# Two of the four latent tiles of a product-key expert layer computed densely instead of by gathered rows

## What is computed

```python
q = (xb @ w_query).reshape(t, PEER_HEADS, 2, HALF_KEY)            # 8 heads, 2 halves of 128
s = einsum('thik,hink->thin', q, sub_keys)                        # 128 keys for each half
v_half, i_half = top_k(s, 16)
cand = v_half[:, :, 0, :, None] + v_half[:, :, 1, None, :]        # 16 x 16 pairs
top_v, top_pos = top_k(cand, 16)                                  # idx = i * 128 + j of the 16 best
g = softmax(top_v)
act = gelu(einsum('thkd,td->thk', expert_u[idx], xb))
out = einsum('thkd,thk->td', expert_v[idx], g * act)
```

## Time and profile before

| | us |
|---|---|
| median of 3 runs | 3107.46 (3094.66 to 3108.46) |
| profiled execution | 3118.87 |
| its span in the profile | 3117.1 |
| busy in the span: PE / VectorE / GpSimd / ScalarE | 2413.1 / 1793.4 / 1572.6 / 667.5 |
| DMA | 819.86 MB, mean 263 GB/s |

### The profile page before, as it was taken

One profiled execution on the slowest core, in us unless ns is written; L12 is line 12 of the kernel. 1 busy time (PEld: TensorE's weight loads), 2 busy tenths in 40 slices (PEclk: granted clock), 3 DMA queues, 4 the chain that ended last, 5 costly groups with the idle time before them and its releaser, 6 DMA issues.

```text
span 3117.1 us, 23624 instructions
## 1 busy us (share of the span) xinstructions
PE 2413.1 (77%) x7124; PEld 1185.1 (38%) x7124; DVE 1793.4 (58%) x3673; ACT 667.5 (21%) x1493; POOL 1572.6 (50%) x1376
## 2 busy tenths in 40 slices
PE   7988888999999958967557886766766676667667
PEld 1444554444565424754223342322222232222223
DVE  0347677431115775877876656656666666666552
ACT  0114435221111112111212122121212121221122
POOL 0011222210001333874458667777777777777775
PEclk9799999999999979988778998888988888898898
DMA  8411111140655665997689999999999999999997
GB/s 292 145 48 35 30 44 36 66 152 26 229 182 189 201 230 194 381 416 259 220 292 337 336 351 366 382 363 363 366 371 372 374 374 385 369 378 356 360 361 293
DMA packets 285385, 819.86 MB, mean 263 GB/s; under 512 B 24929, under 2 KB 68065, under 8 KB 285153
## 3 DMA queue, kind: packets, MB, share of 16 engines
q0 software_dynamic: 184320, 671.17, 57.5%
q1 hardware_dynamic: 100960, 147.43, 13.7%
HBM read 813.79 MB, written 4.72 MB: 263 GB/s over the span
## 4 chain that ended last, share of the span: by engine, by line
PE 19%; POOL 16%; DMA 9%; issue 6%; DVE 4%; ACT 1%; SPq 0%; ACTq 0%; POOLq 0%
PE bank L917 14%; POOL arena L1290 9%; POOL arena L1279 8%; DMA arena<-in_peer_u,arena 4%; DMA arena<-in_peer_v,arena 3%; PE bank L886 2%; DVE arena L1610 2%; DMA arena<-in_keys 1%; PE bank L729 1%; DVE arena L1627 1%; ACT arena L1202 0%; PE bank L897 0%; PE bank L744 0%; DVE arena L1617 0%; PE bank L562 0%
## 5 line engine op out<-in xcount | busy, mean ns | idle before, releaser
L917 PE MATMUL bank<-arena 128*128 128x512 f32 x2048 | 995.1, 636 | 422.4 <-ACT arena L1202 339.3
L1279 POOL DMA_INDIRECT arena<-in_peer_u,arena x640 | 711.8, 1112 | 734.0 <-DVE arena L1603 297.6
L1610 DVE CUSTOM_DVE_ANT_0 arena<-arena 128x1024 f32<-128x1024 f32 x640 | 771.0, 1224 | 526.1 <-DMA arena<-in_peer_u,arena 525.9
L1290 POOL DMA_INDIRECT arena<-in_peer_v,arena x640 | 745.4, 1165 | 244.2 <-issue 164.1
L917 PEld LDWEIGHTS bank<-arena 128*128 128x128 f32 x2048 | 402.5, 203 | 1003.4 <-issue 604.9
L729 PE MATMUL bank<-arena 128*128 128x512 f32 (+1 forms) x1600 | 564.1, 515 | 14.5 <-DMA arena<-in_w_in 3.8
L729 PEld LDWEIGHTS bank<-arena 128*128 128x128 f32 x1600 | 307.4, 193 | 266.4 <-issue 226.6
L1202 ACT ACTIVATE arena<-shape_consts,arena 128x128 f32<-128x128 f32 x512 | 195.0, 399 | 923.9 <-PE bank L917 642.8
L583 PE MATMUL bank<-arena 128*128 128x512 f32 x384 | 183.9, 626 | 7.8 <-ACT arena L972 6.5
L1627 DVE SCALAR_TENSOR_TENSOR arena<-arena 128x1024 f32<-128x1024 f32 x127 | 163.7, 1289 | 30.1 <-DMA arena<-in_peer_v,arena 29.1
L1259 POOL TENSOR_TENSOR arena<-arena 128x512 f32<-128x512 f32 x40 | 45.4, 1135 | 266.1 <-ACT arena L1020 266.1
(11 more groups left out here) (203 smaller groups left out, 2065.0 us busy)
## 6 DMA issues: line engine op xcount, KB each, us to landing
arena<-in_w_in SPq DMA_DIRECT2D x22, 2048.0 KB, 8.2
arena<-in_w_ada SPq DMA_DIRECT2D x12, 2048.0 KB, 7.8
arena<-in_w_ssd_out SPq DMA_DIRECT2D x8, 2048.0 KB, 7.7
arena<-in_peer_u,arena POOLq DMA_INDIRECT x640, 6.2
arena<-in_peer_v,arena POOLq DMA_INDIRECT x640, 6.3
arena<-in_w_fourier SPq DMA_DIRECT2D x4, 2048.0 KB, 7.5
arena<-in_w_out SPq DMA_DIRECT2D x4, 2048.0 KB, 13.2
arena<-in_w_query SPq DMA_DIRECT2D x4, 2048.0 KB, 7.7
```

The costliest lines, as they stand in the source:

```text
L917: last = mm(bank[i][:, :], diag[:, m % 4, :], vrow[V_SLOT[k]][:, 512 * i:512 * i + 512], start=(h == 0 and m == 0), stop=(h == PH - 1 and ...
L1279: nc.gpsimd.indirect_dma_start(urow[U_SLOT[k]], None, a["peer_u"], bass.IndirectOffsetOnAxis(ap=entries(IDX, k), axis=0)).then_inc(u_in[U_ ...
L1290: nc.gpsimd.indirect_dma_start(vrow[V_SLOT[k]], None, a["peer_v"], bass.IndirectOffsetOnAxis(ap=entries(IDX, k), axis=0)).then_inc(v_in[V_ ...
L1610: V.tensor_tensor_reduce(out=urow[slot], in0=urow[slot], in1=h2c, scale=1.0, scalar=0.0, op0=ALU.mult, op1=ALU.add, accum_out=dots[item % ...
```

## The change

Tiles 1 and 2 (`APART`) stay gathered. Tiles 3 and 4 (`WHOLE`, 256 tokens) go through all 16,384 experts densely:
- `s_block(i)`: for each of the 128 blocks of 128 experts PE makes u-block times h2 of both tiles (8 matmuls of 128x256), ScalarE takes GELU of it into `Aw` (64 blocks at a time fit). u comes as a copy of `peer_u` laid out for this, `peer_ut`, made before launch.
- The gate: selections keep indices i and j and the softmax weight as tables, which PE turns (`turn_tables`). In 32 units of 8 tokens, for each half of the i range: VectorE compares i with a row of numbers (`equal_i`), ScalarE scales by the weight (`weigh_i`), GpSimd makes the one-hot of j (`hot_units`, 8 `tensor_scalar` of 128x128), PE multiplies them, one 64-column matmul a token (`build_unit`), and VectorE multiplies the result into `Aw` (`gate_unit`).
- `v_block(i)`: PE adds `Aw` of block i times v-block (4 matmuls of 128x512) into four banks.

PE's order is: all queries and scores, score blocks of the first half, the build of its gate, then v block and second-half score block in turn 64 times, the second build, 64 v blocks. Blocks of 0.5 MB come over SP's queue into six slots.

For tiles 1 and 2 the sum with v is now made by VectorE (`v_add`), not by PE, with 4 (later, for u, another 4) slots for each; u runs 40 steps ahead of v. GpSimd and VectorE take these 296 steps in fixed portions: 20 beside the selections, 20 before the first build, 1 or 2 in each of the 32 units, 86 between, again 48 in the second build, the rest at the end. The latent queries take whole loads of w_query (jobs `Q0` to `Q3`) and 128x256 matmuls, twice as many. Outputs are stored from ScalarE's queue.

```diff
@@ constants
+APART, WHOLE = (1, 2), (3, 4)
+U_SLOT = [k % 4 for k in range(PICKS + 32)] + [2 + k % 4 for k in range(PICKS + 32, GATHERED)]
+V_SLOT = [k % 4 for k in range(GATHERED)]
+APART_LEAD = 40
+APART_BUILD = [1 + u % 2 for u in range(UNITS)]
+APART_BETWEEN = 86
...
@@ tensor
+            for half in range(2 * PH):
+                queries(half, 0)
+                queries(half, 1)
+                if half >= 2 and half % 2 == 0:
+                    scores(half // 2 - 1)
+            scores(PH - 1)
...
+            def build_unit(g, u):
+                n = UNITS * g + u
+                pe.wait_ge(s("ihot_done"), n + 1)
+                pe.wait_ge(s("jhot_done"), n + 1)
+                if n >= 2:
+                    pe.wait_ge(s("g_done"), n - 1)
+                for t in range(UNIT):
+                    last = mm(bank[6 + u % 2][:, HALF * t:HALF * t + HALF], hot_j[u % 2][:, t, :], hot_i[u % 2][:, t, :],
+                              start=True, stop=True)
+                last.then_inc(s("g_full"), 1)
...
+            for n, i in enumerate(FIRST_ORDER):
+                s_block(i)
+                if n == 58:
+                    turn_tables()
+            pe.wait_ge(s("tw_out"), 1)
+            for u in range(UNITS):
+                build_unit(0, u)
+            pe.wait_ge(s("g_done"), UNITS)
+            for i in SECOND_ORDER:
+                v_block(i)
+                s_block(HALF + i)
+            for u in range(UNITS):
+                build_unit(1, u)
+            pe.wait_ge(s("g_done"), 2 * UNITS)
+            for i in SECOND_ORDER:
+                v_block(HALF + i)
...
@@ gpsimd
+            def rows_of_apart(n):
...
+                    if j < 2 * PICKS:
+                        if j % TOPK == 0:
+                            pool.wait_ge(s("topk_done"), PH + j // TOPK + 1)
+                        if j == 32:
+                            pool.wait_ge(s("out_done"), 16)
+                        u_row(PICKS + j)
+                    if j >= APART_LEAD:
+                        v_row(PICKS + j - APART_LEAD)
+            def hot_units(g, u):
+                n = UNITS * g + u
+                if n >= 2:
+                    pool.wait_ge(s("g_full"), n - 1)
...
+                for t in range(UNIT):
+                    last = nc.gpsimd.tensor_scalar(hot_j[u % 2][:, t, :], iota, turned_w[:, 1, UNIT * u + t:UNIT * u + t + 1],
+                                                   None, ALU.is_equal)
+                last.then_inc(s("jhot_done"), 1)
+            def build(g):
+                hot_units(g, 0)
+                hot_units(g, 1)
+                for u in range(UNITS):
+                    rows_of_apart(APART_BUILD[u])
+                    if u + 2 < UNITS:
+                        hot_units(g, u + 2)
...
@@ vector
+            def equal_i(g, u):
...
+                TT(hot_i[u % 2], iota[:, HALF * g:HALF * g + HALF].unsqueeze(1).broadcast_to([P, UNIT, HALF]),
+                   turned_w[:, 0, UNIT * u:UNIT * u + UNIT].unsqueeze(2).broadcast_to([P, UNIT, HALF]),
+                   ALU.is_equal).then_inc(s("ieq_done"), 1)
+            def gate_unit(g, u):
...
+                part = Aw[:, :, UNIT * u:UNIT * u + UNIT]
+                TT(part, part, bank[6 + u % 2][:, :].rearrange("p (t i) -> p i t", t=UNIT), ALU.mult).then_inc(s("g_done"), 1)
+            def build(g):
+                equal_i(g, 0)
+                equal_i(g, 1)
+                for u in range(UNITS):
+                    apart_steps(APART_BUILD[u])
+                    gate_unit(g, u)
+                    if u + 2 < UNITS:
+                        equal_i(g, u + 2)
+            context_steps(4)
+            for h in range(PH):
+                top(3 * PH + h)
+                top(4 * PH + h)
+                context_steps(CTX_BESIDE[h])
+                if h in APART_TOP_BESIDE:
+                    top(PH + APART_TOP_BESIDE[h])
+                apart_steps(APART_BESIDE[h])
+            result(0, pv_c, row(3, 0), 1, 0)
+            apart_steps(SOFTMAX_AT)
+            weigh_whole()
+            apart_steps(APART_EARLY - SOFTMAX_AT)
+            dve.wait_ge(s("tw_out"), 1)
+            build(0)
+            apart_steps(APART_BETWEEN)
+            build(1)
+            apart_steps(ASTEPS)
```

More of the change, by code:

```diff
@@ L519, in _ @@
+            for n in range(len(BLOCKS)):
+                load_block(n)
+            sp.wait_ge(s("out_done"), 16 * NT)
             sp.wait_ge(s("cst_out"), NG * 32 + 16)
@@ new lines, in queries @@
+            def queries(half, pair):
+                n = 2 * half + pair
+                if half % 4 == 0 and pair == 0:
+                    need(JOB["l", f"Q{half // 4}"])
+                if n >= 4:
+                    pe.wait_ge(s("fq_out"), n - 3)
+                w = ring[JOB["l", f"Q{half // 4}"] % 2].rearrange("p (k c) -> p k c", k=KT)
+                c0 = half % 4 * P
+                for k in range(KT):
+                    last = mm(bank[n % 4][:, 0:2 * P], w[:, k, c0:c0 + P], h2Tp[1 - pair][:, k, :],
+                              start=(k == 0), stop=(k == KT - 1))
+                last.then_inc(s("fq_full"), 1)
@@ new lines, in v_block @@
+            def v_block(i):
+                number = B_NUMBER["v", i]
+                pe.wait_ge(b_in[B_SLOT[number]], 16 * B_TURN[number])
+                v = blocks[B_SLOT[number]]
+                for t in range(2):
+                    for half in range(2):
+                        last = mm(bank[2 * t + half][:, :], Aw[:, i % HALF, t * P:t * P + P], v[:, 512 * half:512 * half + 512],
+                                  start=(i == 0), stop=(i == NKEY - 1), skip_group_check=True)
+                last.then_inc(s("av_done"), 1)
@@ new lines, in _ @@
+            for n, i in enumerate(FIRST_ORDER):
+                take_s(n, i)
+                if n == 30:
+                    act.wait_ge(s("vc_used"), PICKS)
+                    tile_norm(0, pv_c, h2c)
+                if n == 46:
+                    act.wait_ge(s("topw_done"), 2 * PH)
+                    A(d_w, d_w, ACT.Exp).then_inc(s("ew_done"), 1)
+                for item in APART_GATES.get(("first", n), []):
+                    gates(item)
+                if n == 54:
+                    store(0, 1)
@@ new lines, in _ @@
+            for u in range(UNITS):
+                weigh_i(1, u)
+                if u == UNITS // 4:
+                    store(1, 2)
+                for item in APART_GATES.get(("build", 1, u), []):
+                    gates(item)
+            for item in APART_GATES.get(("last",), []):
+                gates(item)
+            act.wait_ge(s("vc_used"), 3 * PICKS)
+            act.wait_ge(s("topk_done"), 3 * PH)
+            tile_norm(2, pv_a[1], scratch[:, 0:D])
+            store(2, 3)
+            act.wait_ge(s("av_done"), NKEY)
@@ L1240, in _ @@
+            store(3, 4)
+            store(4, 5)
         @block.gpsimd
@@ L1602, in top @@
                 ch(V.tensor_reduce(pick, eq, AX.X, ALU.add))
-                STT(entries(IDX, item * TOPK, TOPK), pick[:, 0:16], float(NKEY), pick[:, 16:32],
-                    ALU.mult, ALU.add).then_inc(s("topk_done"), 1)
+                if t in WHOLE:
+                    for half in range(2):
+                        last = CP(ij_w[half][:, t - 3, TOPK * h:TOPK * h + TOPK], pick[:, 16 * half:16 * half + 16])
+                    last.then_inc(s("topw_done"), 1)
+                else:
+                    STT(entries(IDX, item * TOPK, TOPK), pick[:, 0:16], float(NKEY), pick[:, 16:32],
+                        ALU.mult, ALU.add).then_inc(s("topk_done"), 1)
             def u_dot(k):
@@ L1762, in _ @@
[L1762 to L1775 removed]
+                make_h2(t, mix(t), h2a[:, t - 1, :] if t in APART else mix(t))
@@ new lines, in _ @@
+            result(0, pv_c, row(3, 0), 1, 0)
[3 more added lines that the diff above has]
+            dve.wait_ge(s("tw_out"), 1)
+            build(0)
+            apart_steps(APART_BETWEEN)
+            build(1)
+            apart_steps(ASTEPS)
+            result(2, pv_a[1], row(3, 1), 3, 2)
+            for t in WHOLE:
+                dve.wait_ge(s("pv_done"), 3 + t)
+                n = t
+                ch(V.reciprocal(pstat[:, n, 2:3], pstat[:, n, 3:4]))
+                for half in range(2):
+                    part = slice(512 * half, 512 * half + 512)
+                    ch(STT(pv_a[0][:, part], bank[2 * (t - 3) + half][:, :], pstat[:, n, 2:3], row(3, 1)[:, part],
+                           ALU.mult, ALU.mult))
+                TT(x1(t), pv_a[0], x1(t), ALU.add).then_inc(s("out_ready"), 1)
```

480 lines of the change are left out of this document (298 added, 182 removed).

## The result

| | us |
|---|---|
| kernel before, median | 3107.96 (3094.66 to 3108.57) |
| changed kernel, median | 3312.50 (3307.48 to 3314.86) |
| ratio | 1.067, 95% interval 1.063 to 1.070 |
| span of the profiled execution, before / after | 3117.1 / 3305.7 |

What follows compares the result with a forecast made beforehand. Gather bandwidth was taken to bound the kernel's last 1,500 us. Adding PE's order, 1891 + 269 + 450 + 5 + 269 + 245 + 19 gave a span of 3148 us, scaled to a median of 3138; range 3025 to 3290.

Steps and rivals of the forecast that it cites:

- first one-hots and build: Before the middle: 6 us for tables and first one-hots in the 9, then 32 units of 8.4 us, 269 us.
- middle: Between the builds: 64 pairs of v product and score block at 6.88 us, plus 10, 450 us; transfers barely covered.
- second build: After the middle: 5 us to fill, then 32 units of 8.4 us, 269 us.
- last products, gathers: After the second build: PE needs 220 us, 90 MB of rows and blocks 243; 245 taken, gathers ending last.
- tail: From the last product to the end: norm and result of tile 2, then the dense tiles' output, 19 us.
- dear one-hots: Rival in the builds: GpSimd's tensor_scalar at 0.65 us, a unit of 11.2 us, 3317 us in all; chance 0.20.
- Meetings: In the builds: GpSimd operations wait for two-input VectorE operations, 11 at 0.21 us, 2.3 us a unit.
- feeding fails: Rival in middle and end: longer landings make PE wait for blocks; up to 3280 us, 3210 likelier; chance 0.10.
- The wait of 9 us in `gates(7)`: In the queries: ScalarE, at the ninth half head, waits about 9 us for the last context dots.
- Break-even: In the builds: the change neither gains nor loses at a unit of 7.9 us, or a tensor_scalar of 0.24.
- three signs of being wrong: tensor_scalar starts under 0.5 us apart on average; a build under 250 us; PE waiting over 10 us for blocks in the middle.
- cheap one-hots: Rival in the builds: the loop between engines paces them, 7.1 us a unit, 3055 us in all; chance 0.30.

Runs made afterwards that it cites:

- e3: The changed kernel with no gathered steps in the two builds (145 instead of 86 in the middle, the rest after the second build): 3134.6 us, ratio 0.992.
- e6: e2 with 20 of the 96 gathered steps moved out of the builds, 19 of them into the middle: 2956.3 us, ratio 0.931.
- e2: The changed kernel with the one-hots of j made by one VectorE comparison of 128x1024 a unit, not by GpSimd: 3007.3 us, ratio 0.952.
- e11: The changed kernel with two GpSimd comparisons of 128x512 a unit in place of eight of 128x128, timing only: 3130.8 us, one run.

## Why the prediction was wrong in size

The sign and the place were right, the time wasn't: 3138 forecast, 3312 measured, 22 above the range's end. Step by step, in span:

| step | predicted | measured | difference |
|---|---|---|---|
| start of the queries | 1518.6 | 1528.7 | +10 |
| queries, scores | 135 | 126 | -10 |
| first scores | 228 | 222 | -6 |
| first one-hots and build | 9 + 269 | 379 | +101 |
| middle | 450 | 443 | -7 |
| second build | 5 + 269 | 368 | +94 |
| last products, gathers | 245 | 223 | -22 |
| tail | 19 | 16 | -3 |

These sum to +157, the whole miss in span (3148 against 3306). The other 17 us of the 174 come from scaling to the median: I took 12 us off for it, and the changed kernel's profiled execution was 5 below its own median.

- **The failed step** is the size of one term, the `tensor_scalar` of GpSimd: 0.30 us taken, 0.60 measured alone (e3), so 4.8 us a unit for 2.4. It stands on the engine that paces both builds. The first build's unit of 11.8 us is then 4.8 for comparisons, 4.0 for 3.25 gathers at 1.24, 2.6 of meetings (2.4 in the comparisons, 0.2 in the gathers) and 0.4 at the start; predicted were 2.4, 3.7, 2.3 and nothing. With 0.60 in my own sum the unit is 10.8 and the time 3292. That this comes within 20 us of 3312 is partly luck: the builds took 195 us more than predicted, of which this term explains 154, and the other steps together took 38 less. The rival "dear one-hots" at 0.65 gave 3317, the right mechanism and nearly the time; I gave it 0.20 and let the range end inside it.
- Why 0.30: the only row was a multiply of 128x512 in 1.04 us, and I read from its gapless successor that little of it is fixed. The comparison has a fixed part of 0.28 us all the same, and a column of it costs 2.5 ns where the multiply with all it includes costs 2.0. Here the cost by the column didn't carry over from one operation to another, and two instructions without a gap say nothing on what is fixed inside each.
- **Meetings** were right in sum: 2.3 us a unit from the stretch of the gathers, 2.6 measured, and in e3, where `equal_i` is nearly all the two-input work beside them, they shrink to 0.04 us a comparison. In their parts two misses cancel: I had 0.21 us for each of 11 operations, and a comparison waited 0.30, a gather 0.07. That VectorE would be idle a third of a build was short: it was idle a half, since the unit grew and its work didn't.
- **PE's pace** was right everywhere: 64 score blocks took 222 us, 3.47 each, 64 pairs 443, 6.92 each, and the middle had no wait for blocks, so the rival "feeding fails" fell. The wait of 9 us in `gates(7)` did not occur.
- **The last stretch** was shorter, and full on both sides: PE had no gap, and I had priced 90 MB at 371 GB/s where with both queues the engines moved 391 (401 in e6's middle). The row with 415 was the nearer one. PE's last matmul ended at 3289.8 us, but the tail still hangs on the last gathered row, as predicted: its product (L1884) ended at 3287.4, then came tile 2's norm on ScalarE (L1358) and its result on VectorE (L2026), and only then ScalarE's squares of the dense tiles (L1440):

```profile
3287.44 1.06 ACT L1358 ACTIVATE arena<-arena 128x1024 f32<-128x1024 f32 x1 [83.73 <-DVE arena L1884]
...
3293.39 0.60 ACT L1440 ACTIVATE arena<-bank 128x512 f32<-128x512 f32 x1 [3.20 <-DVE arena L2026]
```

- **Break-even** was put at a unit of 7.9 us and lies higher, since the rest of the kernel came out shorter: e2 has 7.1 and 6.9 us and takes 3007, e11 has 8.9 and 9.1 and takes 3131. A line between them reaches the 3108 of the kernel before at 8.6 (an estimate), and the 3154 that this kernel took beside e11 at more than e11's own 9.0.
- Of the signs written down ahead, the shape held (holes of PE at 3, GpSimd at 9, DMA below half), and the sizes didn't: holes of 370 instead of 270 us, a comparison alone at 0.60 instead of 0.3, the queries at 1529 instead of 1518. None of the three signs of being wrong came about; the two on the builds looked only at the cheap side.
- Slips in the working that change nothing above: of the slices from the middle on, the 21st is at 8 and the last at 7 tenths, not 9; the terms of the loop in "cheap one-hots" add up to 18.2, not 18.5 (7.0 us a unit); the middle of the bounds 0.13 and 1.04 is 0.59, not 0.65 (3284 us instead of 3317).
- Of the late start of the queries, 10 us in the first profile and 6 to 21 in all, only this is shown: it comes with every kernel that has the change, and 7.9 of the first profile's 10.1 us are longer waits of PE for loads of the mixer's weights (38.7 us against 30.8). Why they land later stays open.

## What to carry to other kernels

Price an instruction form that the trace doesn't show from a row of the same operation and size, or keep the whole bound as the case; a form repeated 512 times on the engine that everything waits for deserves the dear end of it. Here the engine that issues the gathers was a bad place for compute: what it computes delays the rows, its waits for buffers stand ahead of them, and two-input work on VectorE holds it up as well; one wide comparison on VectorE (1.23 us) replaced eight on GpSimd (7.2 us) and took 305 us off the changed kernel, from slower than the kernel before to faster. Then move transfers out of the stretch whose engine is full into one whose DMA engines still have room.

## What was unexpected of the hardware

- GpSimd's comparison with one input costs 0.28 us and 2.5 ns a column (128x64 0.44, 128x128 0.60, 128x512 1.55 us), more than its two-input multiply of 128x512 (1.04 us). VectorE makes the 128x128 form in 0.27, starting one every 0.21.
- Nearly all of a meeting is paid by GpSimd: comparisons went from 0.60 to about 1.15 us beside a dot or product, while those took 1.26 and 1.31 us in the changed kernel's builds against 1.21 and 1.28 in e2's.
- Gathers alone moved 347 to 370 GB/s in two profiles of the kernel before, which took 3108 to 3173 us in the median (2%) from chip to chip; gathers and block loads together 391 to 407.
- PE's granted clock fell to 0.50, the 1.2 GHz level, in every build, where PE did short matmuls in bursts of 3.7 us with gaps between them (mostly 5 to 9 us in the changed kernel, about 1.2 in e3), and was back at 1.00 in the changed kernel's middle. In the changed kernel GpSimd waited 4.1 us for PE in the first build, so the slow clock cost next to nothing there.
